# Expert items taken two at a time with one gather per pair in split fp32r, part of the loop written out, and SBUF buffers placed at multiples of 64 bytes

## The reference

```python
def moe_swiglu(x, router_w, w_gate, w_up, w_down):      # 8 experts, top 2, width 3584
    logits = (x @ router_w).astype(jnp.float32)
    top_v, top_i = lax.top_k(logits, TOP_K)
    gates = jax.nn.softmax(top_v, axis=-1)
    combine = jnp.sum(jax.nn.one_hot(top_i, N_EXPERTS, dtype=jnp.float32) * gates[..., None], axis=-2)
    y = jnp.zeros_like(x)
    for e in range(N_EXPERTS):
        y = y + combine[..., e:e + 1].astype(x.dtype) * swiglu(x, w_gate[e], w_up[e], w_down[e])
    return y
```

## Time and profile before

| | |
|---|---|
| median of 3 runs | 2152.03 us (2149.94 to 2154.01) |
| profiled execution | 2157.44 us, its span 2154.8 us |
| share busy | PE 97%, weight loads 77%, DVE 70%, ACT 47%, POOL 2% |
| the largest group, splits of pieces on DVE | 548.7 us (L2650, ring) and 219.7 us (L2650, more_raw) |
| mean granted TensorE clock | 0.974 of full speed |
| HBM | 499.96 MB read, 233 GB/s over the span |

### The profile page before, as it was taken

One profiled execution on the slowest core, in us unless ns is written; L12 is line 12 of the kernel. 1 busy time (PEld: TensorE's weight loads), 2 busy tenths in 40 slices (PEclk: granted clock), 3 DMA queues, 4 the chain that ended last, 5 costly groups with the idle time before them and its releaser, 6 DMA issues.

```text
span 2154.8 us, 28044 instructions
## 1 busy us (share of the span) xinstructions
PE 2088.3 (97%) x10596; PEld 1665.9 (77%) x10596; DVE 1510.5 (70%) x1837; ACT 1006.0 (47%) x1082; POOL 50.9 (2%) x56
## 2 busy tenths in 40 slices
PE   7999999999998999999889999999999999999996
PEld 4786677756876799888747888888888888888885
DVE  4565434554597445438848888898888889888887
ACT  1121312122133334313236777777777777677674
POOL 0000000000011000000200000000000000000000
PEclk9998999999999999999988999999999999999999
DMA  9844043611621265452127999999999999999990
GB/s 356 279 140 159 30 146 99 226 43 38 217 79 40 92 202 196 172 183 81 44 107 291 395 355 368 347 355 372 330 374 337 367 346 355 376 327 375 333 368 20
DMA packets 238710, 502.18 MB, mean 233 GB/s; under 512 B 11275, under 2 KB 53027, under 8 KB 238627
## 3 DMA queue, kind: packets, MB, share of 16 engines
q1 hardware_dynamic: 238626, 501.03, 65.0%
HBM read 499.96 MB, written 1.05 MB: 233 GB/s over the span
## 4 chain that ended last, share of the span: by engine, by line
PE 89%; DVE 7%; ACT 2%; issue 1%; DMA 0%; SPq 0%; DVEq 0%; ACTq 0%
PE bank L1506 12%; PE bank L1489 9%; PE bank L1491 9%; PE bank L1490 9%; PE bank L757 6%; PE bank L1196 6%; PE bank L989 3%; PE bank L1064 3%; PE bank L765 3%; PE bank L1166 3%; PE bank L1433 3%; PE bank L1172 2%; PE bank L1404 2%; PE bank L1403 2%; PE bank L1402 2%; PE bank L1368 2%
## 5 line engine op out<-in xcount | busy, mean ns | idle before, releaser
L2650 DVE TENSOR_TENSOR ring_r<-ring,his 128x2048 fp32r<-128x2048 f32 x240 | 548.7, 2290 | 77.9 <-ACT his L1619 77.2
L1619 ACT ACTIVATE his<-ring 128x2048 fp32r<-128x2048 f32 x240 | 460.2, 1918 | 127.5 <-PE bank L1491 74.7
L1489 PE MATMUL bank<-his,xe_hi 128*128 128x512 f32 x896 | 354.1, 395 | 0.2 <-DVE ring_r L2650 0.2
L1491 PE MATMUL bank<-his,xe_lo 128*128 128x512 f32 x896 | 349.5, 390 | 0.0
L1490 PE MATMUL bank<-ring_r,xe_hi 128*128 128x512 f32 x704 | 274.2, 389 | 0.0
L2650 DVE TENSOR_TENSOR more_raw_r<-more_raw,his 128x2048 fp32r<-128x2048 f32 x96 | 219.7, 2290 | 27.5 <-ACT his L1619 27.4
L1619 ACT ACTIVATE his<-more_raw 128x2048 fp32r<-128x2048 f32 x96 | 184.2, 1919 | 54.6 <-PE bank L1506 29.1
L1489 PEld LDWEIGHTS bank<-his,xe_hi 128*128 128x128 f32 x896 | 168.2, 188 | 37.0 <-DVE ring_r L2650 3.3
L1491 PEld LDWEIGHTS bank<-his,xe_lo 128*128 128x128 f32 x896 | 168.2, 188 | 35.9
L1490 PEld LDWEIGHTS bank<-ring_r,xe_hi 128*128 128x128 f32 x704 | 132.3, 188 | 26.7
L1196 PE MATMUL bank<-uT,ring 128*128 128x256 f32 (+1 forms) x768 | 149.1, 356 | 0.0
(11 more groups left out here) (439 smaller groups left out, 3093.4 us busy)
## 6 DMA issues: line engine op xcount, KB each, us to landing
ring<-in_moe_w_gate_dram SPq DMA_DIRECT2D x96, 1024.0 KB, 5.2
ring<-in_moe_w_up_dram SPq DMA_DIRECT2D x80, 1024.0 KB, 5.3
ring<-in_moe_w_down_dram SPq DMA_DIRECT2D x64, 1024.0 KB, 4.9
more_raw<-in_moe_w_down_dram SPq DMA_DIRECT2D x48, 1024.0 KB, 5.0
ring<-in_w_in_dram SPq DMA_DIRECT2D x16, 2048.0 KB, 11.4
more_raw<-in_moe_w_up_dram SPq DMA_DIRECT2D x32, 1024.0 KB, 5.2
ring<-in_w_ada_dram SPq DMA_DIRECT2D x12, 2048.0 KB, 10.8
ring<-in_w_out_dram SPq DMA_DIRECT2D x8, 2048.0 KB, 9.6
```

The costliest lines, as they stand in the source:

```text
L1489: mm(bank[b][:, :], xe_hi[:, k, :], hi[:, kk, :], start=(k == 0), stop=False)
L1491: last = mm(bank[b][:, :], xe_lo[:, k, :], hi[:, kk, :], start=False, stop=(k == KD - 1))
L1619: return go(out, in_, ACT.Copy, scale=scale)
L2650: tt(piece_lo(s), piece_raw(s), piece_hi(s).bitcast(fp32), ALU.subtract).then_inc(S("lo_ready"), 1)
```

## The change

1. **Pairs.** Items are taken in pairs m with two members a = 0, 1. `pick` holds 256 columns, 128 for each member, in fp32r. One gather serves the pair; it runs in the odd member's chunk 5, and the even member's chunk 5 has none.
2. **Split gather.** The input x is split once into `x_hi` (ScalarE) and `x_lo` (VectorE, written over x). For each of four groups f of 256 features, 4 fp32r matmuls of 256 columns gather x_hi to one bank and 4 gather x_lo to another. The copies to `xe_hi` and half of those to `xe_lo` are ScalarE's, the other half VectorE's. Groups wait for the copies of the group before.
3. **Order in chunk 5** of an odd member: group 0, a down piece, group 1, a down piece, group 2, an up piece, group 3, an up piece.
4. **Start.** The scaling of the residual (`total`, four instructions) and the split of x move ahead of the router's results on VectorE; `combine` and `list_items` both stand between chunks -2 and -1.
5. **Straight code.** The first two pairs (`STRAIGHT = 2`) and the last one are written out, the loop between takes a pair per turn. SyncE loads the first two pairs' weights without the item list. The last norm's rows are loaded after the last up piece.
6. **Buffers** start at multiples of 64 bytes (`sb` adds 32 bytes of filling); `xe_lo`, `ye_lo`, `x_hi`, `x_lo` lie over `lng`/`lnb`, constants and x that are used no more, and the constants' order is changed for that.

```diff
+            made = place[0].enter_context(nc.sbuf_tensor(name, shape, dtype))
+            if name not in ("lnst", "lnmv") and 0 < math.prod(shape[1:]) * 4 % LINE <= LINE // 2:
+                place[0].enter_context(nc.sbuf_tensor(f"{name}_fill", [P, LINE // 8], fp32))
...
             for s in range(RAWS):
                 if s < 2 * RING:
                     slot_free(sp, loads[len(loads) - RING + s // 2][0])
-                elif s == 2 * RING:
-                    norm_rows(sp, NORMS - 1, A["ln_ffn_g_2"][1], A["ln_ffn_b_2"][1])
                 load_piece(s, bass.ds(0, 1))
...
+            sp.wait_ge(S("piece_used"), m * (2 * NPIECE) + (NPIECE + chunk_at(4) + 4))
+            norm_rows(sp, NORMS - 1, A["ln_ffn_g_2"][1], A["ln_ffn_b_2"][1])
...
+            def gather(m, f, lo, b):
+
+                if f and not lo:
+                    pe.wait_ge(S("xe_hi_ready"), m * 4 + f)
+                elif f:
+                    pe.wait_ge(S("xe_lo_even" if f % 2 else "xe_lo_odd"), m * 2 + (f + 1) // 2)
+                src = x_lo if lo else x_hi
+                for kk in range(2):
+                    k = 2 * f + kk
                     for i in range(NT):
+                        last = mm(bank[b][:, kk * 2 * P:(kk + 1) * 2 * P], src[:, i, k * P:(k + 1) * P], pick[:, i, :],
+                                  start=(i == 0), stop=(i == NT - 1))
+                last.then_inc(S("gathered_lo" if lo else "gathered_hi"), 1)
...
+            def first_up(n, a, m, s0, b):
+
+                for half in range(2):
+                    if half:
+                        gather_both(m, 3)
+                    pe.wait_ge(S("xe_hi_ready"), m * 4 + (2 * half + 2))
+                    pe.wait_ge(S("xe_lo_even"), m * 2 + (half + 1))
+                    pe.wait_ge(S("xe_lo_odd"), m * 2 + (half + 1))
+                    up_piece(n, a, s0 + half, half, b)
...
                 if j == 5:
                     turn_hidden(g - 1)
+                if j == 5 and a == 1:
                     pe.wait_ge(S("picks_copied"), n + 1)
-                    pe.wait_ge(S("picked"), n + 2)
-                    gather(0)
+                    pe.wait_ge(S("picked"), m + 2)
+                    gather(m + 1, 0, False, 5)
                     pe.wait_ge(S("he_ready"), g)
-                    gather(1)
+                    gather(m + 1, 0, True, 4)
+                    down_piece(n, s0)
+                    gather_both(m + 1, 1)
+                    down_piece(n, s0 + 1)
+                    gather_both(m + 1, 2)
+                    first_up(n, to, m + 1, s0 + 2, b)
+                    s0 += 2
+                elif j == 5:
                     down_pieces(n, g - 1, s0)
...
+                        if j == 5 and a == 1 and r in (1, 2, 3, 4):
+                            gathered_hi(m + 1, r - 1, 5)
...
+                for i in range(NT):
+                    dve.wait_ge(S("x_hi_ready"), i + 1)
+                    dve.wait_ge(S("acc_added"), 2 * i + 2)
+                    tt(x_lo[:, i, :], x[:, i, :], x_hi[:, i, :].bitcast(fp32), ALU.subtract).then_inc(S("x_lo_ready"), 1)
```

More of the change, by code:

```diff
@@ L61 @@
 KE = D_FE // P
+LINE = 64
 RING = 5
@@ L136, in constants @@
     later["level0"] = lv[:, 0].T.copy()
+    later["tri_le"] = (row <= col).astype(np.float32)
+    later["tri_lt"] = (row < col).astype(np.float32)
+    later["iota"] = np.broadcast_to(r[None, :], (P, P)).astype(np.float32)
+    parts["fill"] = np.zeros((P, -sum(v.shape[1] for v in parts.values()) % 64), np.float32)
     at = {}
@@ L541, in build @@
         his = sb("his", [P, HIS, PIECE], fp32r)
[L542 removed]
+        xe_hi = sb("xe_hi", [P, 2, KD, P], fp32r)
         he_hi, he_lo = sb("he_hi", [P, 4, P], fp32r), sb("he_lo", [P, 4, P], fp32r)
@@ L730, in _ @@
[L730 to L733, removed]
-                    load_piece(s, bass.ds(e[piece_of(s)[1]], 1))
[L735 to L738, removed]
+            more = sp.value_load(items[0:1, 4 * NE:4 * NE + 1], min_val=NE // 2 - 1 - STRAIGHT, max_val=NE - 1 - STRAIGHT)
@@ new lines, in _ @@
+            with sp.Fori(0, more) as turn:
+                m = turn + STRAIGHT
+                e = [sp.value_load(items[0:1, bass.ds(turn * 2 + (2 * (NE + STRAIGHT) + after), 1)], min_val=0, max_val=NE - 1)
+                     for after in range(3)]
+                for s in range(RAWS, RAWS + 2 * NPIECE):
+                    sp.wait_ge(S("piece_used"), m * (2 * NPIECE) + (s - RAWS + 1))
+                    load_piece(s, bass.ds(e[piece_of(s)[1]], 1))
+            m = more + STRAIGHT
+            e = [sp.value_load(items[0:1, bass.ds(more * 2 + (2 * (NE + STRAIGHT) + after), 1)], min_val=0, max_val=NE - 1)
+                 for after in range(2)]
@@ new lines, in gather_both, with down_piece @@
+            def gather_both(m, f):
+                gather(m, f, False, 5)
+                gather(m, f, True, 4)
+            def down_piece(n, s):
+                half, q = piece_of(s)[3], piece_of(s)[2]
+                pe.wait_ge(S("lo_ready"), n * NPIECE + (s + 1))
+                hi, lo = piece_hi(s), piece_lo(s)
+                for kk in range(2):
+                    k = 2 * half + kk
+                    for a, w in ((he_hi, hi), (he_hi, lo), (he_lo, hi)):
+                        for c in range(2):
+                            last = mm(bank[6 + c][:, :], a[:, k, :], w[:, kk, 512 * c:512 * c + 512],
+                                      start=(q == 0 and k == 0 and a is he_hi and w is hi),
+                                      stop=(q == NQ - 1 and k == 3 and a is he_lo))
+                last.then_inc(S("piece_used"), 1)
@@ L2679, in experts @@
                 for i in range(NT):
-                    last = ts(pick[:, i, :], C("iota"), places[:, i, 0:1], None, ALU.is_equal)
+                    for a in range(2):
+                        last = ts(pick[:, i, a * P:(a + 1) * P], C("iota"), places[:, i, a:a + 1], None, ALU.is_equal)
                 last.then_inc(S("first_pick"), 1)
@@ new lines, in combine, with pick_tokens @@
+                    link(nc.vector.tensor_copy(comb[:, :, NE:2 * NE], comb[:, :, 0:NE]))
+                    nc.vector.tensor_copy(combc[:, :, :], comb[:, :, 0:2]).then_inc(S("picked"), 1)
+                def pick_tokens(m):
+                    for a in range(2):
+                        if isinstance(m, int) and 2 * m + a < NE:
+                            c = 2 * m + a
+                        else:
+                            c = dve.value_load(items[0:1, bass.ds(m * 2 + a, 1)], min_val=0, max_val=2 * NE)
+                        for i in range(NT):
+                            ts(pick[:, i, a * P:(a + 1) * P], C("iota"), places[:, i, bass.ds(c, 1)], None, ALU.is_equal)
+                            last = nc.vector.tensor_copy(combc[:, i, a:a + 1], comb[:, i, bass.ds(c, 1)])
+                    last.then_inc(S("picked"), 1)
```

271 lines of the change are left out of this document (153 added, 118 removed).

## The result

The changed kernel takes 2175.36 us (median of 4 runs, 2173.36 to 2180.45), the kernel before 2153.02 (4 runs beside it). The ratio is 1.0102, 95% interval 1.0086 to 1.0119: 22 us slower, where 6.5 were forecast and the range ended at 2165.

What follows compares the result with a forecast made beforehand. TensorE, 89% of the span, was taken as the bound. Start +6.3, even members -7.2 and odd members +7.4 gave +6.5 us, so a median of 2158.5 us, with a range of 2147 to 2165.

Steps and rivals of the forecast that it cites:

- scalings, subtractions, comparisons at the start: VectorE work ahead of the routing, +1.8 us after cover by idle time; two more comparisons for `pick`, +0.5 us.
- first gather: Gather at the start: 32 matmuls at the low clock, 7.7 us against 5.71 before, +2.0 us.
- combine and list ahead of the fifth piece: `combine` and a longer item list between two VectorE splits at the start delay the fifth piece, +2.0 us.
- even member's chunk 5, each of four: No gather, but down pieces still wait for `he_lo`: hole 2.02 us instead of 3.83, -1.81 each, -7.2 together.
- odd member's chunk 5, each of three: Pair's gather plus a wait for ScalarE's last copies: 6.28 us against 3.83, +2.45 each, +7.4 together.
- straight code: Writing four items out in the expert loop gives 0, since the old loop's turn showed no stall.
- Buffers. [...] I take 0, bounds -1 and +1: New buffer places cost nothing, judged by two ScalarE copies of 597 and 596 ns; 0 us, bounds -1 and +1.
- The rival on buffers: Multiples of 64 speed VectorE and ScalarE up in the first 1128 us; kernel at 2145 us, chance 0.10.
- The sign of being wrong that I gave: Forecast is wrong if the first 1128 us, up to the routing, move by more than 2 us.
- The rival counts five turns: Straight code gives back a stall at each of five loop turns, 2.2 us each; 2147 us, chance 0.03.
- The rival that the start would cost little: First gather runs at full clock in 3.84 us, -1.9 in place of +2.0; 2154.6 us, chance 0.27.
- ScalarE wasn't late: Rival: in odd members' chunk 5 group copies queue behind two splits, +6.0 us; 2164.5 us, chance 0.10.

Runs made afterwards that it cites:

- e5: Changed kernel with 192 bytes of filling, so all operands of the experts' matmuls lie 128 past a multiple of 256 again; 2157.86 us, ratio 1.0014 to the kernel before.
- e4: Kernel before with 64 bytes of filling ahead of `xe_hi`, moving the stationary operands and the buffers behind them; 2177.2 us in one run.
- e7: e5 with `STRAIGHT = 0`: the first three pairs are turns of the loop, only the last is written out; 2169.68 us in one run.
- e8: e5 with `combine` moved behind chunk -1 and the item list behind chunk 0 on VectorE; 2158.05 us in one run.
- e1: Changed kernel with 64 bytes of filling ahead of the expert buffers, putting them at multiples of 128; 2170.36 us, ratio 1.0074 to the kernel before.
- e2: Kernel before with 64 bytes of filling ahead of the dense layer's and the experts' buffers, no instruction changed; 2160.92 us, ratio 1.0031.
- e3: Kernel before with 64 bytes of filling ahead of `his` and 64 behind it, which also moved `xe_hi` by 128; 2167.9 us in one run.
- e6: Kernel before with 128 bytes of filling ahead of the expert buffers, moving all operands but `ring`; 2164.1 us in one run.
- m1: Kernel before with everything moved on by 64 bytes, `ring` too, so all expert operands lie 192 past a multiple of 256; 2149.8 us in one run.
- b1: e5 with the pair's gather divided over both members' chunk 5, and the second subtraction and `combine` moved at the start; 2142.90 us, ratio 0.9954 to the kernel before.

## Why the prediction was wrong

The mechanism that I forecast is there, and came near its size. e5 is the changed kernel less the one thing that I had at nothing. Its 2157.9 us beside the forecast 2158.5 is partly luck, since the kernel before was slower beside it (2155.8): by ratio it is 3 us over the kernel before (0.4 to 5.6), and the forecast +6.5 lies just outside that. From the second tile's transposes to the end the profiles give +5.5; with the 1.15 us that the dense layer gains by its new places, which I hadn't in the sum, that is 4.4. The terms:

| term | forecast | measured |
|---|---|---|
| scalings, subtractions, comparisons at the start | +2.3 | +1.8 |
| first gather | +2.0 | +1.2 |
| combine and list ahead of the fifth piece | +2.0 | +2.0 (2.17 waited in e5, 0.16 before) |
| even member's chunk 5, each of four | -1.8 | -1.75 |
| odd member's chunk 5, each of three | +2.45 | +2.6 |
| straight code | 0 | 0 against the short loop |
| dense layer's addresses | 0 | -1.15 |
| norm's rows, loads | 0 | 0: the end after the last transposes is as long as before |
| addresses in the experts | 0, -1 to +1 | +14 to +17 (changed kernel less e5, less the row below; items' periods) |
| clock in the holes | not in the sum | +3.2 (two falls of 1.6) |

The even and the odd terms are read in e5, where the step is that of before: 2.51 against 4.26, and 28.96 us from the first transpose of chunk 5 to those of chunk 6 against 26.39. The scalings and subtractions came at +1.8 as forecast; the 0.5 for two more comparisons didn't come, as the wait for `pick` stayed (1.24 against 1.20).

**The step that failed** is "Buffers. [...] I take 0, bounds -1 and +1". It was worked out from the earlier trace rows, two copies of ScalarE that read a bank and write a buffer at either kind of place. That row says nothing of TensorE, which reads two operands, mostly at the same time: its weight loads are busy for 41 us of the 50 from 1200 on in which its matmuls are. And it is TensorE that bounds the kernel. What the term measured is 4.3 ns on each of 4032 matmuls, +14 to +17 us where I had 0; e5 takes it away with 192 bytes, and e4 brings it about in the kernel before with 64. I took the question to be whether a buffer lies well, for which a comparison of single buffers is the right view, and noted that the expert buffers already lay at multiples of 64. What counts is how they lie to each other, and the change moved five of seven by 64 bytes. Their new distance stood in the allocation order: ring, uT and the first block of constants stay where they were, and the buffers behind the first filling move. The rival on buffers looked for a gain only, and on VectorE and ScalarE; the gain that there is in the first 1128 us, 1.15, is TensorE's. The sign of being wrong that I gave, that stretch moving by more than 2 us, did come (-7.4), but for the other part of it by the clock.

**Second, straight code.** The number, 0, held, but the reason was incomplete. (The rival counts five turns that are gone; it is all six, since the new loop's body runs once. Nothing hangs on it.) What the prediction draws from the Trainium skill ("Runtime: NRT & Kernel Launch", Instruction fetch mechanics) leaves out a condition of that page: it tells the stall of a target page that isn't on hand, so a turn without a stall doesn't speak against it. The earlier trace rows show a turn of the loop of one item. The change's loop has two items in its body, and e7 shows that this loop stalls at its turn. I should have asked what the new loop's turn costs, not only what the old one's did. It didn't count because with four pairs the loop's body runs once, and no stall like e7's stands in the changed kernel's trace.

**Third, the clock.** The even member's hole, 1.9 us without a matmul, wasn't looked at as more than a wait. In two of the four (items 2 and 6) the granted clock fell to 0.52, the 1.2 GHz level, for 3.4 us directly behind it (the fourth stretch above), and the down pieces took 1.6 us more. Five kernels have four such holes each. It fell behind two of them in the changed kernel, behind two in e8, and behind none in e1, e5 and e7, 4 of 20; e7's one fall came behind a stop at the second turn of its loop, the one of 3.45 us from start to start. In the six with the old gather in seven of eight chunks 5 (before, e2, e3, e4, e6, m1) and in b1 it never fell in the experts ahead of the last item's end. So it is a cost that comes and goes, and it was seen only in kernels with stops of 1.9 us and more. That the stops are its cause isn't shown, nor that b1 owes its freedom to the filled holes, since e5 had no fall either.

The rival that the start would cost little was half right: the gather took 6.9 us, between 3.8 at full clock and 7.7 at half, and its last matmuls went at full clock (0.74 us a group where the first took 1.22). ScalarE wasn't late. Of the changed kernel's time, step and clock make the whole difference to my forecast: 16 + 3 on top of 6.5 is 25 where 22 was measured; the dense layer's 1.15 comes off it.

## What to carry to other kernels

When a change moves buffers, write down where each operand of the bounding matmuls lies before and after modulo 256, and compare the start-to-start step of one matmul form. The engine's busy share said nothing here (50.00 of 50 us in both), and the record's duration little (395 ns became 400). Work that was put into a wait that existed anyway was free: count what fits into the hole first (16 matmuls of 0.12 us into 2 us), and only then whether there should be fewer of them. A doubled loop body can have its own price at the turn, which the trace of the shorter loop can't show.

## What the runs showed of the hardware

- fp32r matmuls of 512 columns, busy TensorE at full granted clock: 227.4 ns from start to start when both operands of all matmuls in turn lie at the same place modulo 256 bytes of a partition (at 128, or at 192), 229.6 to 233.3 otherwise. Within one kernel the step goes with the operands (227.4 to 233.5 by kind in e6). In the kernel before, with no instruction changed, unequal places cost 8 to 21 us by the profiles (e2, e3, e4, e6). Why is open: whether the loading of the next stationary operand and the reading of the moving one meet in memory wasn't tested. Nor was every place tried: all at a multiple of 256 would be one, a distance under 64 bytes another.
- The rule doesn't carry over to 256 columns. In the dense layer a median of 119 to 120 ns for all three products of before became 118, 122 and 114 with unequal places, which is faster on the whole (137.77 us became 135.65). fp32 matmuls kept their 429 and 215 ns.
- The turn of the loop with the instructions of two items (e7) stopped TensorE for 4.2 and 4.7 us, that of one item not at all.
- The stretch up to the second tile's transposes has the same instructions and buffers in six profiles (changed kernel, e1, e5, e7, e8, b1) and took 1117.7 to 1125.2 us. The time lost to the lower granted clock in it was 33.3 us in the shortest (b1) and 41.9 in the longest (e7).
